# Splitting the first layer's input products by token halves and running its recurrence beside them

## The chip, the core and the metric

The kernel runs on one core of one Trainium2 chip, all in float32. Times are device microseconds of one launch. Before the change the median of three runs is 2656.42 us (2653.24 to 2658.45). TensorE is called PE in the profile, VectorE DVE, ScalarE ACT, GpSimd POOL and SyncE SP; TensorE's clock has two levels here, 1.2 and 2.4 GHz, given as a granted clock of 0.5 and 1.

## What is computed

The reference runs two transformer layers over 512 tokens of width 1024 and then a third block of another kind. The change lies in the first layer's mixer, a gated linear recurrence over chunks of 16 tokens with 8 heads of 128:

```python
proj = xn @ w_in                       # [512, 4096] = q | f | i | g
fgate = lbf + (1 - lbf) * sigmoid(f);  log_f = log(fgate);  k = 1 - fgate
q = silu(q);  v = i
def step(state, (qc, kc, vc, lfc)):    # one chunk of 16 tokens
    cum = cumsum(lfc);  last = cum[-1]
    qd, kd = qc * exp(cum), kc * exp(-cum)
    scores = where(causal, qd @ kd.T, 0)
    o = scores @ vc + qd @ state
    state = exp(last) * state + (kc * exp(last - cum)).T @ vc
o = o * rsqrt(mean(o * o) + eps) * onorm_g * silu(g)
h = h + gate * (o @ w_out)
```

`xn` is the normed input, scaled and shifted by columns of modulation vectors. All of these (17 x 1024 numbers) are products of the condition vector with matrices of 1024 rows; the kernel computes those of later layers beside the first layer's products too.

## The kernel before

The stages follow one another, each in a block with a barrier at its end. Within a block every engine runs its own list of instructions in order and waits for semaphores.

`first_loads` loads constants and `h`, and starts the first slabs of the modulation matrices (`vring`, GpSimd's DMA queue). `project` (L187) is the general routine: TensorE runs a list of jobs, each a group of matmuls into one PSUM bank with weights from a ring of three 2 MB slabs (`load_slab`, L160, on SyncE's queue), ScalarE or VectorE evacuates, and, where `vectors` is given, VectorE multiplies matrix slabs of 1024 x 256 by the condition vector (`vector_parts`, L291 and L295, eight instructions for a group of 256 columns), GpSimd reloads the ring of three 1 MB slabs (L182), and TensorE sums the 128 partitions of a finished group with one-column matmuls (`vector_sums`, L239). Eight groups of partial sums can be pending (`NPART`).

`project("mods_a")` makes the first two vectors, without jobs. `norm_to_xT` norms `h` and turns it into `xT` (channels on partitions). `project("hgrn_in")` runs 32 jobs of 512 columns over 8 slabs: q and f by channel (`by_column`, all 512 tokens moving), v and g by tile of 128 tokens (`by_token`), all evacuated by ScalarE; 60 vector groups lie beside them.

`hgrn` (L487) is the recurrence, four tiles of 128 tokens. A schedule by (tile, step), the same on all three engines, orders it: LOG (ScalarE's Ln of the gate), CUM (VectorE's scans and differences), EXPS (three Exp), PREP (VectorE multiplies them into q and keys), REACH to REACH+8 (VectorE builds the keys as seen from each chunk into one of three buffers, TensorE forms the chunk's scores of all heads, 16 passes), TURN (VectorE masks the scores, chain of chunk decays; TensorE turns the keys), OUT (TensorE's outputs and the state's increment, ScalarE's evacuation, VectorE's state), SUM, ROOT (Ln and Exp on ScalarE), GATE. The next tile's CUM to PREP is put between TURN and SUM of this one.

`turn_to_xT` transposes the gated output, `make_rows` spreads four gate vectors over the partitions (rows), and `project_back` runs 8 output jobs of 512 columns; VectorE adds them, gated, to `h` (L406, L407). Then come the experts and all the rest, which the change leaves as it is but for the numbers of two slabs in the ring.

## Time and profile before

| | us |
|---|---|
| median of the timed runs | 2656.42 |
| profiled execution | 2656.48 |
| its span in the trace | 2654.7 |
| TensorE busy | 2072.0 (78%) |
| VectorE busy | 1683.3 (63%) |
| ScalarE busy | 789.3 (30%) |
| GpSimd busy | 620.0 (23%) |
| end of the output products of the first layer | 541.8 |

A busy share is an average over stages with different limits; matmuls are pipelined, so that a busy TensorE isn't one at its peak. In a timeline line the first number is the start, the second the length of the merged group, "x16" the number of instructions in it, and what stands in brackets is the idle time before it and what ended that. A group of matmuls ends with the drain of its last one, about 0.17 us.

### The profile page before, as it was taken

To read this page: it belongs to the slowest core of one execution; us is meant where nothing else is said; L and a number is where in the kernel's file an instruction comes from. 1 tells how busy PE (TensorE), PEld (TensorE's weight loads), DVE (VectorE), ACT (ScalarE), POOL (GpSimd) and SP (SyncE) were. 2 spreads that over 40 slices of the span, in tenths; PEclk is the share of its full clock that TensorE was granted. 3 is DMA by queue.
4 is the path that set the end of the run, shared out by engine and by line. 5 is a ranking of instruction groups with operands and counts; after the bars stand their busy time and mean duration, and the time that the engine had idled before them with its cause. 6 is when DMAs were issued, how large, how long until landed. Compare 5 with 4: busy or idle time off the path is not lost. (4 is left out here: it accounts for less than half of the span.)

```text
span 2654.7 us, 30433 instructions
## 1 busy us (share of the span) xinstructions
PE 2072.0 (78%) x11214; PEld 1224.0 (46%) x11214; DVE 1683.3 (63%) x3993; ACT 789.3 (30%) x1736; POOL 620.0 (23%) x589
## 2 busy tenths in 40 slices
PE   2999776857776689888789888867887859856787
PEld 1454376443322146555256445523433436636664
DVE  5888875238978677554676753467885424954442
ACT  1100132123332332543343553335232242131221
POOL 0111000014444433433332233233344300000000
PEclk9999866979878699989799898877999969986889
DMA  7788600029999999999899888889999923310000
GB/s 299 286 315 326 239 1 1 32 96 421 420 419 421 422 416 413 407 391 387 358 371 392 302 333 302 337 351 350 420 418 419 420 104 112 93 74 1 9 9 16
DMA packets 111189, 723.58 MB, mean 273 GB/s; under 512 B 12080, under 2 KB 15024, under 8 KB 34880
## 3 DMA queue, kind: packets, MB, share of 16 engines
q0 software_dynamic: 84000, 610.65, 57.7%
q1 hardware_dynamic: 27040, 110.98, 11.1%
q8 instruction: 89, 1.46, 0.2%
q14 instruction: 60, 0.49, 0.0%
HBM read 718.18 MB, written 3.41 MB: 272 GB/s over the span
## 5 line engine op out<-in xcount | busy, mean ns | idle before, releaser
L1494 PE MATMUL ps<-got,diag 64*64 64x512 f32 x4096 | 640.1, 715 | 315.4 <-ACT diag L1565 293.5
L1515 POOL DMA_INDIRECT got<-in_peer_uv,idx x512 | 581.1, 1135 | 980.8 <-PE ps L1494 878.8
L1600 DVE CUSTOM_DVE_ANT_0 got<-got,xk 128x1024 f32<-128x1024 f32 x512 | 615.9, 1222 | 272.7 <-DMA got<-in_peer_uv,idx 262.3
L1494 PEld LDWEIGHTS ps<-got,diag 64*64 64x64 f32 x4096 | 127.5, 148 | 623.8 <-ACT diag L1565 516.6
L1560 ACT ACTIVATE gelu<-eye,hid 128x64 f32<-128x64 f32 x512 | 176.5, 345 | 689.3 <-DVE hid L1600 684.5
L1128 PE MATMUL ps<-xT,ring 128*128 128x256 f32 x928 | 225.3, 394 | 6.6 <-DVE qkv L1217 6.6
L1128 PEld LDWEIGHTS ps<-xT,ring 128*128 128x128 f32 x928 | 174.5, 194 | 85.5 <-issue 46.7
L295 DVE SCALAR_TENSOR_TENSOR hgrn_in_psums<-vring,vec,hgrn_in_psums 128x256 f32<-128x256 f32 x420 | 203.6, 485 | 15.0
L1565 ACT ACTIVATE diag<-gelu,gate 128x64 f32<-128x64 f32 x512 | 178.0, 348 | 54.6 <-PE ps L1494 6.6
L830 PE MATMUL ps<-xT,ring 128*128 128x256 f32 x768 | 190.2, 397 | 0.3 <-ACT xT L943 0.3
L830 PEld LDWEIGHTS ps<-xT,ring 128*128 128x128 f32 x768 | 144.0, 195 | 76.5 <-issue 47.1
L256 PE MATMUL ps<-ring,xT 128*128 128x512 f32 x384 | 169.0, 596 | 1.4 <-PEq L459 1.4
L859 PEld LDWEIGHTS ps<-ring,xT 128*128 128x128 f32 x1024 | 118.4, 192 | 44.8 <-issue 36.7
L859 PE MATMUL ps<-ring,xT 128*128 128x128 f32 x1024 | 128.9, 280 | 0.0
L256 PE MATMUL ps<-xT,ring 128*128 128x512 f32 x256 | 113.3, 597 | 1.2 <-PEq L356 1.2
L256 PEld LDWEIGHTS ps<-ring,xT 128*128 128x128 f32 x384 | 71.7, 190 | 85.9 <-issue 85.9
L182 POOL DMA_DIRECT2D vring<-in_vslabs x68 | 36.1, 532 | 271.6 <-DVE hgrn_in_psums L291 202.9
L256 PEld LDWEIGHTS ps<-xT,ring 128*128 128x128 f32 x256 | 47.6, 190 | 56.0 <-issue 56.0
L1471 PEld LDWEIGHTS ps<-xT,ring 128*128 128x128 f32 x512 | 59.9, 194 | 24.3 <-issue 17.0
L1471 PE MATMUL ps<-xT,ring 128*128 128x128 f32 x512 | 64.6, 282 | 2.4 <-PEq L356 1.2
L2129 PE MATMUL ps<-w_out,xT 128*128 128x512 f32 x128 | 61.2, 628 | 0.8 <-DVE xT L2275 0.8
L1506 POOL IOTA iota<- 128x16 f32 x1 | 0.1, 135 | 249.5 <-POOLq L356 249.5
(497 smaller groups left out, 2494.5 us busy)
## 6 DMA issues: line engine op xcount, KB each, us to landing
ring<-in_small SPq DMA_DIRECT2D x142, 512.0 KB
vring<-in_vslabs POOLq DMA_DIRECT2D x68, 1024.0 KB, 5.2
ring<-in_slabs SPq DMA_DIRECT2D x12, 2048.0 KB, 9.4
got<-in_peer_uv,idx POOLq DMA_INDIRECT x512
w_out<-in_slabs SPq DMA_DIRECT2D x2, 2048.0 KB, 11.0
h<-in_x SPq DMA_DIRECT2D x1, 2048.0 KB, 16.6
out<-h SPq DMA_DIRECT2D x4, 512.0 KB, 2.6
bias_rows<-brow POOLq DMA_DIRECT2D x1, 1280.0 KB, 4.8
```

The costliest lines, as they stand in the source:

```text
L256: mm = nc.tensor.matmul(o, l, r, start=start, stop=end)
L295: ins = nc.vector.scalar_tensor_tensor(acc, part, one, acc, ALU.mult, ALU.add)
L830: mm = nc.tensor.matmul(bank[:, 0:2 * P], w[:, k, :], xT[:, k, own], start=(k == 0), stop=(k == ND - 1))
L859: mm = nc.tensor.matmul(bank[:, P * half:P * half + P], x[:, k, P * half:P * half + P], w[:, k, :], start=(k == 0), stop=(k == ND - 1))
L1128: mm = nc.tensor.matmul(bank[:, 0:2 * P], w[:, k, :], xT[:, k, own], start=(k == 0), stop=(k == ND - 1))
L1471: mm = nc.tensor.matmul(ps[:, bank, P * half:P * half + P], slab(f + g)[:, k, c:c + P], xT[:, k, P * w:P * w + P], start=(k == 0), stop=(k ...
L1494: mm = nc.tensor.matmul(ps[to:to + HALF, i, :], diag[own, n % NDIAG, :], got[own, n % GRING, 1, 512 * g:512 * g + 512], start=(k == 0), st ...
L1515: nc.gpsimd.indirect_dma_start(out=got[:, n % GRING].rearrange("p a d -> p (a d)"), out_offset=None, in_=table, in_offset=bass.IndirectOff ...
L1560: nc.scalar.activation(gelu_of[:, n % 2, :], eye2[:], ACT.Gelu, scale=hid[:, w % 2, k:k + 1]).then_inc(gelu_done, 1)
L1565: nc.scalar.activation(diag[:, i, :], gelu_of[:, n % 2, :], ACT.Copy, scale=gate[:, w % 2, k:k + 1]).then_inc(diag_ready, 1)
L1600: nc.vector.tensor_tensor_reduce(row_in, row_in, xk[:, w % 2, :], 1.0, 0.0, ALU.mult, ALU.add, hid[:, w % 2, k:k + 1]).then_inc(dotted, 1)
L2129: mm = nc.tensor.matmul(ps[:, 4 * (t % 2) + 2 * part, :], xT[:, j, P * t:P * t + P], w_out[:, part, j, :], start=(j == 0), stop=(j == ND - 1))
```

## The change

- A vector group has 512 columns, not 256, and is loaded in four pieces of 2 x 128 rows (0.5 MB each); the ring holds five pieces, and two groups of partial sums can be pending.
- `hgrn_in` is cut in two. `in_a` runs 32 jobs of 256 columns for tokens 0 to 255 with 14 vector groups, `in_b` 32 such jobs for tokens 256 to 511 with 16 groups. The eight weight slabs are loaded twice.
- The recurrence is cut in halves of two tiles (`hgrn_half`), written as generators that give one step at a time on each engine. The next tile starts 12 steps after the last (`HGAP`). That of tiles 0 and 1 runs beside `in_b`: behind each job every engine does one step, TensorE one job later (`paced`). The products have three PSUM banks, the recurrence four, the vectors one. Its work tiles lie in parts of `xT`, `rows` and `h` that are free then.
- The recurrence of tiles 2 and 3 is a block of its own, into which `beside_hgrn` puts, at every second step, a step of `back_half` for tokens 0 to 255: one gate row, 16 transposes, and 4 output jobs in two chunks of 8 passes each. `h` is loaded again in that block, since it was used as work space.
- A last block makes the other three gate rows and the output jobs of tokens 256 to 511.
- Before its first Ln each half asks for the activation table set with logarithm and exponential.

```diff
-VCOLS = 256
-NVRING = 3
-NPART = 8
+VCOLS = 512
+VK = 2
+NVRING = 5
+NPART = 2
...
+    slabs = in0 + in0 + [q0[0], out0[0], out0[1], None, q0[1]]
+    OUT_SLABS, Q0_SLABS = (17, 18), (16, 20)
...
-                            for k in range(ND):
-                                one, part = cond[:, k:k + 1], vring[:, i % NVRING, k, :]
+                            for k in range(k0, k0 + VK):
+                                one, part = cond[:, k:k + 1], vring[:, i % NVRING, k - k0, :]
...
-            return [(bank[:, :T], w[:, k, c0:c0 + P], (xT if x is None else x)[:, k, :], k == 0, k == ND - 1)
-                    for k in range(ND)]
+            return [(bank[:, :2 * P], w[:, k, c0:c0 + P], xT[:, k, own], k == 0, k == ND - 1) for k in range(ND)]
...
+    def paced(side, lag):
+
+        made = []
+
+        def beside(eng, n):
+            if not made:
+                made.append(side(eng))
+            if n >= lag:
+                next(made[0], None)
+            if n == 31:
+                for _ in made[0]:
+                    pass
+        return beside
+
+    def beside_hgrn(mine, fill):
+
+        for s, _ in enumerate(mine):
+            if s >= 2 and s % 2 == 0:
+                next(fill, None)
+        for _ in fill:
+            pass
...
+                    if k == LOG:
+                        if u:
+                            act.wait_ge(cum_ready, u)
+                        else:
+                            nc.scalar.preload_act_table_set("natural_log_exp_and_others")
...
-            project("hgrn_in", jobs, range(first, len(vslabs)), take_mods(16, NMOD))
-        hgrn(q_all, f_all, v_all, g_all)
-        turn_to_xT("o0", v_all, v("onorm_g"))
-    make_rows()
-    project_back("hgrn_out", "hgrn_out", 0, first_of["out2"])
...
+            project("in_a", half_jobs(0), range(first, middle), take_mods(16, 16 + 4 * 14))
...
+                project("in_b", half_jobs(1), range(middle, len(vslabs)), take_mods(16 + 4 * 14, NMOD), beside=beside,
+                        banks=(4, 5, 6))
...
+                @block.tensor
+                def _(pe):
+                    beside_hgrn(side["pe"](pe), back["pe"](pe))
```

## Rows read from the trace of the kernel before

**Rows 1.** Busy time of each engine by stage; x counts instructions, PEclk is the granted clock.

```profile
core 0: us, PE busy (x) PEld busy (x) DVE busy (x) ACT busy (x) POOL busy (x), PEclk, DMA share, GB/s
0.00:19.30 19.30, 0.00 (x0) 0.00 (x0) 1.58 (x10) 1.72 (x3) 1.94 (x7) 1.00 0.79 303
19.30:51.90 32.60, 8.11 (x32) 7.42 (x32) 29.49 (x65) 0.00 (x0) 4.22 (x8) 1.00 0.69 239
51.90:66.90 15.00, 6.61 (x32) 5.49 (x32) 8.87 (x16) 8.39 (x12) 0.00 (x0) 1.00 1.01 430
66.90:320.90 254.00, 247.39 (x752) 124.73 (x752) 220.50 (x481) 22.96 (x35) 30.16 (x57) 0.99 0.81 304
320.90:467.20 146.30, 93.14 (x696) 90.53 (x696) 103.74 (x270) 49.05 (x51) 0.00 (x0) 0.59 0.00 1
467.20:483.60 16.40, 12.30 (x48) 7.91 (x48) 7.81 (x8) 6.85 (x8) 0.00 (x0) 0.89 0.00 0
483.60:541.80 58.20, 55.17 (x128) 24.24 (x128) 11.06 (x16) 0.00 (x0) 0.00 (x0) 1.00 0.10 36
541.80:2654.70 2112.90, 1649.27 (x9526) 963.65 (x9526) 1300.26 (x3129) 700.37 (x1627) 583.72 (x517) 0.87 0.74 295
```

**Rows 2.** Groups by line and shape, whole run: busy us, mean ns, idle before.

```profile
L291 DVE TENSOR_SCALAR hgrn_in_psums<-vring,vec 128x256 f32<-128x256 f32 x60 | 20.9, 348 | 17.1 <-DMA vring<-in_vslabs 16.7 <-PEq L356 0.4
L295 DVE SCALAR_TENSOR_TENSOR hgrn_in_psums<-vring,vec,hgrn_in_psums 128x256 f32<-128x256 f32 x420 | 203.6, 485 | 15.0
L1802 DVE SCALAR_TENSOR_TENSOR score<-rel,sb_z,score 128x512 f32<-128x512 f32 x7 | 5.3, 752 | 4.3 <-ACT rel L1785 4.1
```

**Rows 3.** Timeline of TensorE, four places: start, length, what, idle before.

```profile
311.55 1.40 PE L239 MATMUL ps<-const,hgrn_in_psums 128*128 128x1 f32 x12
390.44 1.95 PE L599 MATMUL ps<-v_all,hg_kend 128*128 128x128 f32 x16
483.78 55.17 PE L256 MATMUL ps<-ring,xT 128*128 128x512 f32 x128 [1.42 <-PEq L459]
2285.78 31.35 PE L1128 MATMUL ps<-xT,ring 128*128 128x256 f32 x144 [1.73 <-DVE qkv L1217]
```

**Rows 4.** Busy time by stretch inside the recurrence, columns as in the first group.

```profile
320.90:336.20 15.30, 0.00 (x0) 0.00 (x0) 13.75 (x33) 10.20 (x9) 0.00 (x0) 0.50 0.00 0
336.20:353.50 17.30, 17.26 (x136) 17.11 (x137) 13.25 (x42) 2.95 (x3) 0.00 (x0) 0.50 0.01 1
353.50:388.00 34.50, 25.21 (x184) 24.36 (x183) 29.57 (x79) 13.54 (x14) 0.00 (x0) 0.60 0.00 1
```

**Rows 5.** Timeline of the recurrence: tile 0's start, the step between tiles, the end.

```profile
321.10 1.00 DVE L609 TENSOR_SCALAR f_all<-f_all,lb 128x512 f32<-128x512 f32 x2 [0.61 <-PEq L207]
325.95 1.28 ACT L540 ACT_TABLE_LOAD   x1
326.46 2.63 DVE L623 TENSOR_TENSOR_SCAN xT<-hg_starts,xT 128x128 f32<-128x128 f32 x8
336.24 15.77 PE L570 MATMUL ps<-xT,hg_reach 128*16 128x16 f32 x128 [16.07 <-DVE hg_reach L655]
380.17 1.31 DVE L663 COPY_PREDICATED hg_scores<-imask,ps 128x1024 f32<-128x1024 int32 x1 [1.44 <-issue]
414.89 1.31 DVE L663 COPY_PREDICATED hg_scores<-imask,ps 128x1024 f32<-128x1024 int32 x1 [1.44 <-issue]
449.33 1.29 DVE L663 COPY_PREDICATED hg_scores<-imask,ps 128x1024 f32<-128x1024 int32 x1 [7.72 <-issue]
465.81 1.22 DVE L693 TENSOR_TENSOR v_all<-q_all,g_all 128x1024 f32<-128x1024 f32 x1
```

**Rows 6.** Timeline of TensorE in the expert stage, where its clock falls.

```profile
1895.03 1.99 PE L1128 MATMUL ps<-xT,ring 128*128 128x256 f32 x8
1900.77 1.95 PE L1494 MATMUL ps<-got,diag 64*64 64x512 f32 x8 [2.73 <-ACT diag L1565]
1902.65 2.77 PE L1128 MATMUL ps<-xT,ring 128*128 128x256 f32 x8
```

More of the change, by code:

```diff
@@ L99, in vector_plan @@
     wide = [("ada_w", 0, 6), ("ada_w", 1, 6), ("kv_ada_w", None, 2), ("w_ada_2", 0, 3)]
-    return [(name, layer, c) for name, layer, n in wide for c in range(0, n * D, VCOLS)]
+    return [(name, layer, c, k) for name, layer, n in wide for c in range(0, n * D, VCOLS) for k in range(0, ND, VK)]
 def program(nc, io, out):
@@ L182, in load_vslab, with project @@
             eng.dma_start(vring[:, i % NVRING].rearrange("p k n -> p (k n)"), io["vslabs"][i]).then_inc(v_loaded[i % NVRING], 16)
-    NBANK = 6
-    def project(name, slab_jobs, vectors=(), after=None, beside=None, until=None):
+    def project(name, slab_jobs, vectors=(), after=None, beside=None, banks=range(6)):
         jobs = [(i, job) for i, js in slab_jobs for job in js]
@@ L308, in _ @@
                             dve.wait_ge(filled, n + 1)
-                            evac(nc.vector, ps[:, n % NBANK, :], step).then_inc(dve_out, 1)
+                            evac(nc.vector, ps[:, banks[n % NBANK], :], step).then_inc(dve_out, 1)
                         if beside:
@@ L400, in _ @@
                         mm.then_inc(turned, 1)
-    def add_gated(row):
-        def make(t, c0, tmp):
-            def evac(eng, bank, step):
-                step(eng.tensor_tensor(tmp[:, :], bank[:, :WCOLS], rows[:, row, c0:c0 + WCOLS], ALU.mult))
-                return eng.tensor_tensor(h[:, t, c0:c0 + WCOLS], h[:, t, c0:c0 + WCOLS], tmp[:, :], ALU.add)
-            return evac
-        return make
-    def project_back(name, key, row, until):
-        with ExitStack() as st:
-            tmp = sbuf(st, name + "_tmp", [P, WCOLS])
-            make = add_gated(row)
-            first = first_of[key]
-            project(name, [(first + g, [(by_token(t, 0, WCOLS), "dve", make(t, WCOLS * g, tmp)) for t in range(NT)])
-                           for g in range(2)], until=until)
     def root(act, n, x, root_in, root_mid, root_out):
@@ L2348, in build @@
         g_all = sbuf(st, "g_all", [P, NT, D])
+        own_tiles = {n: sbuf(st, "hg_" + n, [P, H, P])[:] for n in ("state", "scores", "kend", "reach0")}
         with ExitStack() as st_v:
-            vring = sbuf(st_v, "vring", [P, NVRING, ND, VCOLS])
+            vring = sbuf(st_v, "vring", [P, NVRING, VK, VCOLS])
             first_loads()
@@ new lines, in build @@
+            project("in_a", half_jobs(0), range(first, middle), take_mods(16, 16 + 4 * 14))
+            with ExitStack() as st_a:
+                quarter = lambda x, t: x[:, :, P * t:P * t + P]
+                flat_tile = lambda x: x.rearrange("p (h x) -> p h x", h=H)
+                tl = dict(own_tiles, logf=quarter(xT, 0), cum=quarter(xT, 1))
+                tl |= {n: flat_tile(rows[:, i, :]) for i, n in enumerate(("ke0", "qd1", "kd1", "ke1"))}
+                tl |= {n: flat_tile(h[:, i, :]) for i, n in enumerate(("qd0", "kd0", "reach1", "reach2"))}
+                side = hgrn_half(st_a, 0, tl, q_all, f_all, v_all, g_all)
+                beside = {}
+                for e, lag in (("pe", 1), ("act", 0), ("dve", 0)):
+                    beside[e] = paced(side[e], lag)
+                project("in_b", half_jobs(1), range(middle, len(vslabs)), take_mods(16 + 4 * 14, NMOD), beside=beside,
+                        banks=(4, 5, 6))
@@ new lines, in build, with _ @@
+        with ExitStack() as st_b:
+            tl = dict(own_tiles, logf=quarter(xT, 2), cum=quarter(xT, 3), qd0=quarter(q_all, 0), kd0=quarter(q_all, 1),
+                      ke0=quarter(f_all, 0), qd1=quarter(f_all, 1), kd1=flat_tile(g_all[:, 0, :]), ke1=flat_tile(g_all[:, 1, :]))
+            tl |= {n: sbuf(st_b, "hg_" + n, [P, H, P])[:] for n in ("reach1", "reach2")}
+            h_again, = sems(st_b, "h_again")
+            side = hgrn_half(st_b, 1, tl, q_all, f_all, v_all, g_all)
+            back = back_half(st_b, 0, v_all, [0], h_again)
+            with nc.Block(no_gpsimd_drain=True) as block:
+                @block.sync
+                def _(sp):
+                    sp.dma_start(h[:], io["x"][0].rearrange("(t p) d -> p t d", p=P)).then_inc(h_again, 16)
+                    sp.wait_ge(h_again, 16)
+                @block.tensor
+                def _(pe):
+                    beside_hgrn(side["pe"](pe), back["pe"](pe))
+                @block.scalar
+                def _(act):
+                    beside_hgrn(side["act"](act), back["act"](act))
+                @block.vector
+                def _(dve):
+                    beside_hgrn(side["dve"](dve), back["dve"](dve))
@@ new lines, in build, with _ @@
+        with ExitStack() as st_c:
+            back = back_half(st_c, 1, v_all, [1, 2, 3], None)
+            with nc.Block(no_gpsimd_drain=True) as block:
+                @block.sync
+                def _(sp):
+                    sp.wait_ge(back["job_done"], 2)
+                    load_slab(sp, OUT_SLABS[0] + NRING)
+                @block.tensor
+                def _(pe):
+                    for _ in back["pe"](pe):
+                        pass
+                @block.scalar
+                def _(act):
+                    for _ in back["act"](act):
+                        pass
+                @block.vector
+                def _(dve):
+                    for _ in back["dve"](dve):
+                        pass
```

588 lines of the change are left out of this document (313 added, 275 removed).

## The prediction

> **What bounds the kernel now.** I first cut the run into the blocks that the code forms and read busy time and granted clock in each [rows 1]. The profiled execution took 2656.48 us, 1.78 more than its span of 2654.7; the median of the three timed runs is 2656.42, so a sum against the profiled run needs no correction. The change touches what ends at 541.8 us; the 2112.9 us behind it keep their instructions and are carried over unchanged. Ahead of it stand seven stages: loads 19.3, first modulation vector 32.6, norm 15.0, input products 254.0, recurrence 146.3, turning plus gate rows 16.4, output products 58.2, together 541.8. The reader is to see three things. The input products are bound by TensorE: 247.4 of 254.0 us busy at full clock, with VectorE at 220.5 beside it on the vector products. The recurrence is bound by nothing that is full: TensorE 93, VectorE 104, ScalarE 49 of 146.3 us, at a granted clock of 0.59. It is a chain that hops between engines. The output products are TensorE alone, 55.2 of 58.2. So overlap has something to win: in 146 us the array does little, and in 254 + 58 us VectorE and ScalarE have room, if VectorE's vector products are made cheaper.
>
> **Unit costs at full clock.** A 512-column pass takes 0.430 us ((55.17 - 0.17)/128; 0.17 is the last one's drain) and a 256-column pass (31.35 - 0.17)/144 = 0.2165 [rows 3]. An f32 matmul is two passes. Hence halving the width costs almost nothing: 1024 narrow passes are 221.7 us where 512 wide ones are 220.0. A half-size job of 16 passes is 3.46 us. A vector column sum is 0.11 us a pass: 1.40 us for 12 [rows 3]; four per old group of 256 columns, eight per new group of 512, so 30 new groups cost what 60 old ones did, 0.89 us each. On VectorE an old group is one 348 ns and seven 485 ns instructions [rows 2], 3.9 us with gaps (the vector stage holds eight in 32.6 us less its 1.3 us tail [rows 1]). The same operation at 512 columns takes 752 ns [rows 2]; with 0.48 for the first (taken between 348 ns and 500 ns, the L609 form over 512 [rows 5]) and small gaps a new group is 5.9 us, 34 of them 201 us where 68 old took 265.
>
> **Part 1, loads and first vector.** The loads block ends when h has landed, and everything in flight shares the rate of 303 GB/s [rows 1]. The new ring holds 5 x 0.524 MB, not 3 x 1.049 MB, so 0.5 MB less lies ahead: -1.7 us, 17.6. The vector stage is 4 x 5.9 + 1.3 = 24.9 if transfers keep up. That asks 0.524 MB per 1.48 us, 354 GB/s, against 239 at a DMA share of 0.69 now, and slab loads start four pieces before the end. I take 25.5 (24.9 to 30). The norm stays 15.0.
>
> **Part 2, input products of tokens 0 to 255.** TensorE: 512 x 0.2165 + 14 groups x 0.89 = 110.8 + 12.5 = 123.3, plus 1.2 of tail. VectorE: 14 x 5.9 = 83, hidden. The transfers are the doubt: 56 vector pieces (29.4 MB) and 8 slabs (16.8 MB, the slabs being loaded twice now) are 46.1 MB, 374 GB/s over 123 us. The input stage now moves 304 GB/s at a share of 0.81, which scales to 375, but the norm's window shows 430 [rows 1]. Only two groups of partial sums are buffered instead of eight, and VectorE already loses 16.7 us to late vector slabs [rows 2]. I take 127 (124 to 136).
> The Trainium skill's page "DMA: Bandwidth & Descriptors", section Specifications, puts the HBM limit of a core at about 358 GB/s; by it the stage would take 46.1/358 = 129 us, an estimate, 2 us over my value. The 430 GB/s row speaks against a limit there.
>
> **Part 3, products of tokens 256 to 511 with the recurrence of tiles 0 and 1.** Products and sums: 110.8 + 16 x 0.89 = 125.0. TensorE's share of the recurrence: at half clock tile 0's 128 score passes take 15.8 us [rows 5], so 7.9 at full; turning, output and state products are 16-pass blocks of 1.8 us at full clock (1.95 for 16 with drain [rows 3]), the turn half of it; tile 0 makes 12.5, tile 1, with a product against the state, 14.4. Sum 152 us. VectorE: 16 x 5.9 = 94.4, and its part of two tiles is 13.75 + 13.25 + 29.6 = 56.6, the busy time from 320.9 to 388.0 [rows 4]: sum 151. Two engines near 150 us that wait for each other step by step: each VectorE job with an even number waits for TensorE's sums of the job before, and TensorE runs step s after job s+1. Walking through the pairs of jobs (TensorE 7.8 us + steps, VectorE 5.9 us + steps) gives three losses. At the start VectorE owes gates and memsets 4.1, scan and differences 5.0, gated keys 3.9 and three pairs' pieces before the first score: it is ready at 28, TensorE at 22.5, 5.5 us. Between the tiles TensorE waits for state copy 1.2, sum 1.4, keys 3.9 and two jobs' pieces 5.9, of which two jobs cover all but 5 us. At the end the last groups and the lag cost 6 to 7 us. Together 170. ScalarE's evacuations (0.4 us) hide; three product banks in place of six suffice, because evacuation runs at most three jobs late in the walk.
> Then the clock. In the expert stage 256-column blocks take 1.99 us, but behind a gap of 2.73 us the next two blocks take 1.95 in place of 1.09 and 2.77 [rows 6]. In the recurrence the score passes leave the clock at 0.50 although TensorE reads 17.26 of 17.3 us busy [rows 4]: narrow passes don't hold it up. Beside the products a score step plus sums is a gap of 1 to 2.5 us between dense jobs, so some falls are likely. Each costs about 1 to 2 us; I take six, 9 us: 179. Bounds are 168 (no fall, fewer waits) and 200.
>
> **Part 4, the block with tiles 2 and 3 and the first output products.** A two-tile recurrence from the present rows: start to the end of the first tile's scores 31.1 (320.9 to 336.24 + 15.77), mask to mask 34.7 (380.17 to 414.89), last mask to end 17.9 (449.33 to 467.2) [rows 5], 83.7. Put into it: 4 output jobs, eight chunks of 8 wide passes, 3.44 us each at full clock; one gate row, 1.7; 16 transposes, 2.6. Of the chunks the one before each mask (VectorE has 4.7 us there), the one behind each output product and the last are covered; four stand in the score steps, where TensorE is full (17.26 of 17.30) [rows 4], 13.8 us bare. That gives 83.7 + 13.8 + 4.3 + 2 of VectorE work = 104; chunks that begin at half clock add some 7, score passes that meet a warm array return 3: 108 (96 to 130). The h reload of 2 MB, now 16.6 us to landing beside others, hides.
> One part is worth 2 to 4 us on paper: each Ln and each Exp reloads its table, 1.28 us [rows 5], twice in a tile's tail. The Trainium skill's "ScalarE: Activation LUTs", section "Table sets: the hidden batching unit", says that one set holds both functions; the new preload asks for it. If that holds, some 3 us leave this block, an estimate; I leave them out of the sum.
>
> **Part 5, the last block.** Three gate rows through one buffer, 3.05 each + 1.1 = 10.3; transposes and evacuation 4.4; 4 jobs x 6.87 = 27.5; last add and block end 3.8: 46 (44 to 50). It replaces, with part 4, the 16.4 and 58.2 of now.
>
> **Sum.** 17.6 + 25.5 + 15.0 + 127 + 179 + 108 + 46 = 518.1, against 541.8: -23.7. 2656.5 - 23.7 = 2632.8, predicted 2633.
>
> **The rivals.** *A, smooth overlap*: clock full throughout, transfers in time: 17.6 + 24.9 + 15 + 124.5 + 169 + 98 + 45 = 494, 2609. For it: VectorE's steps are known and the products are dense. Against: [rows 6]. *B, transfers bind*: the first half takes 136, the vector stage 29, the second half 182: +15.5, 2648. For it the share of 0.81 at 304 GB/s, against it 430 GB/s. *C, overlap in name only*: the engines are coupled in order, each step waits for its slowest partner, and half of the hidden work comes back: second half 190, part 4 120: +23, 2656. The change doesn't do what it says. *D, slower*: the clock falls beside the products. TensorE's 152 us of the second half at a mean clock c last 152/c; with 18 us of waits and c = 0.76 that is 218, and part 4 at half clock throughout 125 (+17): 2689 in full. The total passes 2656 where these two together exceed my values by 24, about c = 0.85. The expert stage with its gaps shows 0.87 [rows 1], which makes this real; against it, TensorE has work nearly always here, and the product stage shows 0.99.
>
> **How the numbers follow.** Forecast 0.55 (2622 to 2648); A 0.17; B 0.10; C 0.08; D 0.10. 0.2%, 5.3 us, is about what a measurement of this kernel can tell from no change. Slower by more takes D: 0.10. Within: C and a little of B: 0.09. Faster: 0.81. The range leaves out part of A below and most of D above: 2602 to 2664.
>
> **What would show it.** The first half at 123 to 130 us with TensorE above 95% busy; wide pass time unchanged; vector groups of 5.9 us. In the second half TensorE above 85% and a granted clock above 0.9; if it is below 0.85, D. In part 4 scores and wide chunks alternating, the block near 108. A long wait for vector pieces in front of L291's successor would be B. If the stages behind move by more than 3 us, the carry-over was wrong.

## The result and the profile after

The changed kernel takes 2617.77 us (median of four runs, 2616.77 to 2626.79) against 2654.83 of the kernel before beside it (2647.89 to 2658.45): a ratio of 0.9871, 95% interval 0.9841 to 0.9901. The predicted 2633 lay on the right side and the time is within the range, but 15 us too high; the time falls below the forecast's own band (2622 to 2648), between it and rival A's 2609. The profiled execution took 2617.68 us and has a span of 2615.7, 39.0 less than before.

Busy time by stage of the changed kernel, columns as in [rows 1]. The stages are loads, first vector, norm, first half of the products, second half with tiles 0 and 1, tiles 2 and 3 with the first output products, the last block, and all the rest.

```profile
core 0: us, PE busy (x) PEld busy (x) DVE busy (x) ACT busy (x) POOL busy (x), PEclk, DMA share, GB/s
0.00:18.30 18.30, 0.00 (x0) 0.00 (x0) 1.57 (x9) 1.71 (x3) 2.98 (x9) 1.00 0.78 291
18.30:46.70 28.40, 7.46 (x32) 7.12 (x32) 22.88 (x33) 0.00 (x0) 8.47 (x16) 1.00 0.83 303
46.70:61.80 15.10, 7.01 (x32) 5.92 (x33) 8.85 (x15) 8.42 (x13) 0.00 (x0) 1.00 0.96 402
61.80:188.10 126.30, 123.92 (x624) 110.59 (x625) 80.21 (x113) 16.07 (x35) 29.59 (x56) 0.99 0.92 348
188.10:368.10 180.00, 164.27 (x992) 146.20 (x992) 143.35 (x267) 45.73 (x65) 31.41 (x59) 0.94 0.76 279
368.10:465.80 97.70, 71.42 (x428) 49.72 (x428) 60.01 (x155) 17.50 (x23) 0.00 (x0) 0.78 0.06 22
465.80:514.30 48.50, 39.22 (x92) 16.85 (x92) 10.87 (x15) 4.64 (x8) 0.00 (x0) 0.89 0.12 44
514.30:2615.70 2101.40, 1641.20 (x9526) 959.29 (x9526) 1302.20 (x3129) 697.63 (x1625) 581.73 (x517) 0.87 0.74 297
```

| stage | before | forecast | measured |
|---|---|---|---|
| loads | 19.3 | 17.6 | 18.3 |
| first vector | 32.6 | 25.5 | 28.4 |
| norm | 15.0 | 15.0 | 15.1 |
| products, first half | 254.0 for all | 127 | 126.3 |
| second half, tiles 0 and 1 | 146.3 (four tiles) | 179 | 180.0 |
| tiles 2 and 3, first outputs | 16.4 (turning, rows) | 108 | 97.7 |
| last block | 58.2 (outputs) | 46 | 48.5 |
| sum | 541.8 | 518.1 | 514.3 |
| the rest | 2112.9 | 2112.9 | 2101.4 |

So of the 39.0 us in the span 27.5 come from the stages that the change touches (23.7 forecast) and 11.5 from stages whose work it leaves alone (none forecast).

**The second half.** The reader is to see TensorE 91% and VectorE 80% busy in the fifth line: both chains are in there and neither waits much. What TensorE and VectorE waited for in it (us in total, times, longest), first TensorE, then VectorE:

```profile
PE ps L479 <- DVE hg_reach L561: 9.2, 2, 5.0
PE ps L239 <- DVE in_b_psums L296: 5.7, 1, 5.7
```

```profile
DVE in_b_psums L292 <- PE ps L239: 13.4, 6, 2.7
...
DVE in_b_psums L296 <- DMA vring<-in_vslabs: 1.2, 1, 1.2
```

TensorE's three waits are the three of the forecast: before the first scores, between the tiles (two in the first row, 4.14 and 5.04 in the timeline, 5.5 and 5 forecast) and at the tail (5.7; 6 to 7 forecast). VectorE waits for TensorE's sums (L239) six times: each waits on the other, as the walk had it. Transfers cost 1.2 us.

The same stage in stretches of 10 us, columns as before (five of its eighteen):

```profile
188.10:198.10 10.00, 9.97 (x36) 8.42 (x37) 9.13 (x19) 3.96 (x4) 1.58 (x3) 0.77 0.85 342
208.10:218.10 10.00, 5.86 (x42) 4.98 (x40) 8.52 (x12) 0.77 (x2) 2.12 (x4) 0.92 0.96 379
218.10:228.10 10.00, 10.00 (x49) 8.28 (x49) 9.40 (x20) 0.38 (x1) 2.95 (x6) 0.74 0.87 301
288.10:298.10 10.00, 10.00 (x59) 8.08 (x59) 9.51 (x16) 0.76 (x2) 2.11 (x4) 0.82 0.53 197
298.10:308.10 10.00, 10.00 (x74) 8.80 (x72) 8.08 (x18) 0.72 (x3) 2.71 (x5) 1.00 1.00 401
```

The granted clock is below 1 at the block's start, during and behind each of the two waits of 4 to 5 us, in the stretch in which the second of them lies (0.84, row not shown) and in the last (0.76, not shown). In all other stretches it is 1.00, those with score passes of 16 columns between products of 256 among them.

**The block with tiles 2 and 3**, in four stretches: until the first score, first scores to the first mask, mask to second scores, second scores to the second mask. (The end, 16.8 us at a clock of 1.00, isn't shown.)

```profile
368.10:383.00 14.90, 0.00 (x0) 0.00 (x0) 11.76 (x32) 5.29 (x5) 0.00 (x0) 0.50 0.39 141
383.00:404.00 21.00, 20.28 (x149) 17.96 (x149) 9.69 (x28) 3.64 (x6) 0.00 (x0) 0.58 0.00 1
404.00:424.00 20.00, 15.57 (x87) 10.24 (x88) 17.25 (x45) 6.21 (x8) 0.00 (x0) 0.84 0.01 1
424.00:449.00 25.00, 25.00 (x154) 15.37 (x151) 10.48 (x27) 0.00 (x0) 0.00 (x0) 0.92 0.00 1
```

TensorE does nothing in the first, stands at half clock in the second (scores, transposes, one row, no wide chunk), and near full clock in the fourth, where four wide chunks lie between the scores. The chunks in the timeline of TensorE, the first, one of the score stretch and the last:

```profile
404.00 5.51 PE L668 MATMUL ps<-ring,xT 128*128 128x512 f32 x8
...
424.15 5.69 PE L668 MATMUL ps<-ring,xT 128*128 128x512 f32 x8
...
457.37 3.60 PE L668 MATMUL ps<-ring,xT 128*128 128x512 f32 x8
```

Two of the eight begin at half clock and take 5.5 and 5.7 us, the other six 3.6 to 3.7. The four between the second tile's scores are those that begin at 424.15, 431.20, 437.03 and 443.42.

**The last block**, timeline of TensorE:

```profile
467.08 3.78 PE L647 MATMUL ps<-hb_spread,const 128*128 128x512 f32 x4 [6.12 <-DVE hb_spread L695]
472.18 3.78 PE L647 MATMUL ps<-hb_spread,const 128*128 128x512 f32 x4 [1.32 <-DVE hb_spread L695]
477.29 1.98 PE L647 MATMUL ps<-hb_spread,const 128*128 128x512 f32 x4 [1.32 <-DVE hb_spread L695]
480.38 1.97 PE L654 MATMUL ps<-const,v_all 128*128 128x128 f32 x16 [1.11 <-ACT rows L679]
483.71 27.71 PE L668 MATMUL ps<-ring,xT 128*128 128x512 f32 x64 [1.36 <-issue]
```

Three gate rows by turns: two at half clock (3.78 us for four passes), the third at full (1.98). The output products that follow take 27.7 us, 0.430 a pass as in [rows 3].

**The vector groups** of the first half (busy us, mean ns, idle before and what ended it):

```profile
L296 DVE SCALAR_TENSOR_TENSOR in_a_psums<-vring,vec,in_a_psums 128x512 f32<-128x512 f32 x98 | 73.6, 751 | 21.7 <-DMA vring<-in_vslabs 15.5 <-DVE in_a_psums L296 0.5
L292 DVE TENSOR_SCALAR in_a_psums<-vring,vec 128x512 f32<-128x512 f32 x14 | 6.8, 484 | 22.4 <-PE ps L239 11.8 <-DMA vring<-in_vslabs 10.2 <-PEq L356 0.4
```

751 and 484 ns are the 752 and 480 of the forecast. In the first half VectorE stood 25.7 us (15.5 + 10.2) waiting for late pieces, and it cost nothing, since TensorE was busy for 123.9 of 126.3 us.

### The profile page after: what moved, and what is told of

It reads as the page before. It is cut to its first block and busy times, and to the rows that moved or that the text cites. A ratio compares the mean times of both kernels' runs of the same rounds, so it can differ in the third digit from the quotient of the medians.

```text
span 2615.7 us, 31361 instructions
## 1 busy us (share of the span) xinstructions
PE 2054.5 (79%) x11726; PEld 1295.7 (50%) x11726; DVE 1629.9 (62%) x3736; ACT 791.7 (30%) x1770; POOL 654.2 (25%) x657
## 5 line engine op out<-in xcount | busy, mean ns | idle before, releaser
L1151 PE MATMUL ps<-xT,ring 128*128 128x256 f32 x928 | 226.5, 396 | 6.6 <-DVE qkv L1240 6.6
L1151 PEld LDWEIGHTS ps<-xT,ring 128*128 128x128 f32 x928 | 175.3, 195 | 86.4 <-issue 48.3
L853 PE MATMUL ps<-xT,ring 128*128 128x256 f32 x768 | 188.6, 395 | 0.3 <-ACT xT L966 0.3
L853 PEld LDWEIGHTS ps<-xT,ring 128*128 128x128 f32 x768 | 142.9, 193 | 76.2 <-issue 47.3
L184 POOL DMA_DIRECT2D vring<-in_vslabs x136 | 72.2, 532 | 282.9 <-DVE in_b_psums L296 137.8
L882 PEld LDWEIGHTS ps<-ring,xT 128*128 128x128 f32 x1024 | 118.5, 192 | 44.6 <-issue 36.5
L256 PE MATMUL ps<-xT,ring 128*128 128x256 f32 x512 | 119.5, 393 | 2.1 <-PEq L356 1.2
L256 PE MATMUL ps<-ring,xT 128*128 128x256 f32 x512 | 117.3, 387 | 0.0
L256 PEld LDWEIGHTS ps<-xT,ring 128*128 128x128 f32 x512 | 99.2, 197 | 16.0 <-issue 2.4
L256 PEld LDWEIGHTS ps<-ring,xT 128*128 128x128 f32 x512 | 97.2, 193 | 12.7
L296 DVE SCALAR_TENSOR_TENSOR in_b_psums<-vring,vec,in_b_psums 128x512 f32<-128x512 f32 x112 | 84.1, 751 | 8.2 <-DMA vring<-in_vslabs 1.2
L296 DVE SCALAR_TENSOR_TENSOR in_a_psums<-vring,vec,in_a_psums 128x512 f32<-128x512 f32 x98 | 73.6, 751 | 21.7 <-DMA vring<-in_vslabs 15.5
L1493 PEld LDWEIGHTS ps<-xT,ring 128*128 128x128 f32 x512 | 60.4, 195 | 23.8 <-issue 16.5
L668 PE MATMUL ps<-ring,xT 128*128 128x512 f32 x128 | 60.8, 630 | 1.4 <-issue 1.4
## 6 DMA issues: line engine op xcount, KB each, us to landing
got<-in_peer_uv,idx POOLq DMA_INDIRECT x512, 12.5
h<-in_x SPq DMA_DIRECT2D x2, 2048.0 KB, 11.7
```

What stands on the lines that cost most here:

```text
L256: mm = nc.tensor.matmul(o, l, r, start=start, stop=end)
L296: ins = nc.vector.scalar_tensor_tensor(acc, part, one, acc, ALU.mult, ALU.add)
L853: mm = nc.tensor.matmul(bank[:, 0:2 * P], w[:, k, :], xT[:, k, own], start=(k == 0), stop=(k == ND - 1))
L882: mm = nc.tensor.matmul(bank[:, P * half:P * half + P], x[:, k, P * half:P * half + P], w[:, k, :], start=(k == 0), stop=(k == ND - 1))
L1151: mm = nc.tensor.matmul(bank[:, 0:2 * P], w[:, k, :], xT[:, k, own], start=(k == 0), stop=(k == ND - 1))
L1493: mm = nc.tensor.matmul(ps[:, bank, P * half:P * half + P], slab(Q0_SLABS[g])[:, k, c:c + P], xT[:, k, P * w:P * w + P], start=(k == 0), s ...
```

## The experiments

The theory: the gain is two overlaps, each worth more than the halving costs; TensorE and VectorE bound the second half together. The rivals: the gain is the cheaper vector products or the table preload (then the vector format alone has it), the overlap is in name only, or transfers bind.

**The vector format alone.** The kernel before with groups of 512 columns, pieces of 0.5 MB, and nothing else.

```diff
-VCOLS = 256
-NVRING = 3
-NPART = 8
+VCOLS = 512
+VK = 2
+NVRING = 5
+NPART = 2
```

> The kernel before with nothing but the new vector format (groups of 512 columns, four pieces, ring of five, two pending sums). My theory: the vector block loses what the changed kernel's trace shows, 32.6 to 28.4 us and 1.0 us in the loads block, and the input products, bound by TensorE, keep their 254 us less a shorter tail of 2 to 4 us. So 2655 - 8 = 2647 (2643 to 2651). Rival: the cheaper VectorE work by itself carries much of the gain, since the input stage was held by late vector slabs (16.7 us of waits there): then 2635 or below.

It took 2648.97 us, a ratio of 0.9983 (0.9971 to 0.9996): 2.5 us between the medians, 4.5 by the ratio, about as expected. In its trace the front ends at 537.6 instead of 541.8: the first vector takes 27.2 in place of 32.6, the products 253.9 in place of 254.0. The shorter tail that was expected there didn't show. The products were TensorE's, so cheaper work on VectorE gained nothing; it is what makes room for the recurrence.

**The recurrence of tiles 0 and 1 behind the second half.** The changed kernel, where the second half's products run alone and a block of their own holds the two tiles.

```diff
-                project("in_b", half_jobs(1), range(middle, len(vslabs)), take_mods(16 + 4 * 14, NMOD), beside=beside,
+                project("in_b", half_jobs(1), range(middle, len(vslabs)), take_mods(16 + 4 * 14, NMOD),
                         banks=(4, 5, 6))
+                with nc.Block(no_gpsimd_drain=True) as block:
+                    @block.tensor
+                    def _(pe):
+                        for _ in side["pe"](pe):
+                            pass
...
```

> The changed kernel, with the recurrence of tiles 0 and 1 in a block of its own behind the second half's products. My theory: the products fall from 180 to 127 us, and a block of 80 to 84 us comes in: +29, 2647 (2640 to 2655). Rival (overlap in name only): each step waits for its slowest partner and the overlap returns little; then the time stays within 10 us of the changed kernel.

2658.75 us, 1.0023 (1.0009 to 1.0037): slower than before, and above the 2640 to 2655 expected. The two blocks, columns as before, and VectorE's waits for transfers in the first:

```profile
186.50:327.70 141.20, 131.35 (x640) 115.98 (x640) 91.33 (x129) 14.83 (x34) 31.18 (x59) 0.95 0.94 356
327.70:411.80 84.10, 48.79 (x352) 47.69 (x352) 53.71 (x138) 15.82 (x19) 0.00 (x0) 0.58 0.01 2
```

```profile
DVE in_b_psums L296 <- DMA vring<-in_vslabs: 28.4, 8, 6.4
DVE in_b_psums L292 <- DMA vring<-in_vslabs: 10.7, 4, 5.1
```

The two take 225.3 us, beside each other 180.0. The front ends at 555.6, 41.3 later than in the changed kernel. That rules out the overlap in name only. But the products alone take 141.2, not the some 127 that TensorE's work asks for, which is why the expectation was missed: at a DMA share of 0.94 VectorE waits 39 us for pieces. That suggests that this stage, run at TensorE's own pace, is bound by transfers; the rival is that the two pending groups of sums bind it.

**The same with half of the vector traffic of that stage.** From there on every second piece is loaded only in the first 64 columns of one of its two row blocks. All instructions on the engines stay; what the kernel leaves out is data, so that those modulation vectors aren't the reference's.

```diff
+            if i >= 77 and i % 2:
+                eng.dma_start(vring[:, i % NVRING, 0, 0:64], io["vslabs"][i][:, 0:64]).then_inc(v_loaded[i % NVRING], 16)
+                return
```

> The kernel of e2 (recurrence of tiles 0 and 1 alone), in which every second piece of the vector matrices from the second half's products on is loaded only in its first 64 columns of one row block, so those modulation vectors are wrong. In e2 the second half's products took 141 us where TensorE's work is 127, with 39 us of VectorE waits for vector pieces at 356 GB/s. Theory: transfers bind that block; with 15 MB less it falls to 127 to 129 us. Rival: the two pending sums bind it (TensorE and VectorE wait in turn); then it stays near 141.

A single run, 2650.81 us, so the whole time says little; the stage is what counts. The second half's products:

```profile
186.00:315.00 129.00, 127.60 (x640) 113.54 (x640) 92.14 (x130) 14.86 (x34) 31.87 (x59) 0.98 0.73 264
```

129.0 us, TensorE 127.6 of it, 12 us less than above with the same instructions on the engines. So it was the transfers, since the two groups of sums are the same here. Overlapped, the two stages are 45.3 us shorter (225.3 against 180.0; at the front's end it is 41.3, since the stages around them take 4 us less in the trace of the kernel that runs them apart). Some 12 of these are the transfers': with the recurrence beside them they have 180 us for the same bytes. The engines' share is 33 (129.0 + 84.0 against 180.0). Of it about 10 are TensorE's own work becoming shorter, 127.6 + 46.6 us busy apart and 164.3 together: the recurrence alone runs at a clock of 0.58, beside the products the stage has 0.94. The other 23 are idle time that is filled.

**The output products of tokens 0 to 255 in a block of their own**, behind tiles 2 and 3.

```diff
-                    beside_hgrn(side["pe"](pe), back["pe"](pe))
+                    for _ in side["pe"](pe):
+                        pass
...
+            with nc.Block(no_gpsimd_drain=True) as block:
+                @block.tensor
+                def _(pe):
+                    for _ in back["pe"](pe):
+                        pass
...
```

> The changed kernel, with the output products of tokens 0 to 255 in a block of their own behind the recurrence of tiles 2 and 3. My theory: the recurrence alone takes 80 us at a clock near 0.6 (it is 97.7 with them), the outputs alone 36: +18, 2636 (2630 to 2642). Second question: if the wide chunks hold the clock up in the score steps, the block with them should owe less than the 13.8 + 4.3 us that I put on top of the recurrence; then the recurrence alone is nearer 85 than 80.

2644.83 us, 0.9974 (0.9964 to 0.9984), above the 2630 to 2642 expected, because both blocks are longer than the 80 and 36 us assumed; in the trace the front ends at 536.0, 21.7 later. The block of tiles 2 and 3, twenty microseconds of its second score stretch, the new block and the last:

```profile
366.00:452.00 86.00, 46.09 (x344) 45.01 (x344) 52.02 (x142) 14.80 (x18) 0.00 (x0) 0.58 0.07 25
412.00:431.00 19.00, 11.74 (x109) 11.56 (x109) 12.99 (x29) 0.53 (x3) 0.00 (x0) 0.51 0.00 0
452.00:490.70 38.70, 33.16 (x84) 14.98 (x84) 8.41 (x13) 2.60 (x5) 0.00 (x0) 0.94 0.00 0
490.70:536.00 45.30, 35.62 (x92) 15.85 (x92) 10.88 (x15) 4.67 (x8) 0.00 (x0) 0.99 0.13 47
```

The two tiles alone take 86.0 (83.7 was the forecast's base), with the outputs between them 97.7: 38.7 us of other work added 11.7. The scores alone stand at a clock of 0.51; with wide chunks between them their stretch has 0.92. These lines give the second tile's scores, first alone, then with chunks:

```profile
416.95 0.61 PE L479 MATMUL ps<-f_all,hg_reach 128*16 128x16 f32 x16 [7.86 <-DVE hg_reach L561]
419.87 15.35 PE L479 MATMUL ps<-f_all,hg_reach 128*32 128x16 f32 x112 [2.31 <-DVE hg_reach L561]
```

```profile
423.61 0.61 PE L479 MATMUL ps<-f_all,hg_reach 128*16 128x16 f32 x16 [4.43 <-DVE hg_reach L561]
```

Alone they take 18.3 us from the first to the last, 2.3 of it a wait for VectorE, and with four chunks 25.2 (they end at 448.8): 6.9 more, though the four chunks take 16.8. The first tile's stretch is 5.3 longer with a row and the transposes in it (21.1 against 15.8); the pieces between and behind change by under 1 us.

The 97.7 itself isn't fixed. The same block takes 97.6 in the second trace of the changed kernel and 94.8 to 95.7 in three of four traces of kernels that differ only ahead of it, where the clock comes up again within the first tile's scores and they take 18 us to their mask, not 21. The two tiles alone take 87.5 in the trace with both overlaps taken out. So what the outputs add is 7 to 12 us. The last block is 3.2 us shorter here (45.3), at a clock of 0.99: the block ahead of it ends with wide products.

**Both in blocks of their own.** The two edits above together.

> The changed kernel with both overlaps taken out (recurrence of tiles 0 and 1 and the first output products in blocks of their own); only the halves and the vector format remain. If the two gains add, it is the changed kernel's 2618 + 41 (e2) + 27 (e3) = 2686, well above the 2651 of the kernel before. Rival: they share a cause (the clock, the transfers), and the time is under 2676.

2687.24 us, 1.0141 (1.0111 to 1.0172). That is the 2686 expected. The two overlaps add up: in the traces' fronts they return 41.3 and 21.7 taken out one by one, 66.8 (581.1 - 514.3) taken out together. Without them the change is a loss. Against the vector format alone the front is 43.5 us longer (581.1 - 537.6). The input products then take 10 us more (124.0 + 140.3 against 253.9), the recurrence in two halves 23 more (84.4 + 87.5 against 148.7), and what is behind 9 more.

**Without the preload of the table set.**

```diff
                         else:
-                            nc.scalar.preload_act_table_set("natural_log_exp_and_others")
```

> The changed kernel without the request for the activation table set with Ln and Exp. In the changed trace no table is loaded in tile 3's tail nor in the norm that opens the expert stage. My theory: two loads of 1.28 us come back in each of these two places, all others hidden: +5, 2623 (2621 to 2626). Rival: the norm's loads vanished for another reason and the tail's are hidden: no difference.

2621.43 us, 0.9886 (0.9869 to 0.9902); the medians are 3.7 us apart. ScalarE's timeline without it, at the start of the block of tiles 2 and 3, in tile 3's tail and in the next stage's norm (each load at L405 is followed by a second one for the Exp at L407):

```profile
371.29 1.06 ACT L446 ACTIVATE xT<-f_all 128x1024 f32<-128x1024 f32 x1 [1.47 <-DVE f_all L515]
...
456.67 1.28 ACT L405 ACT_TABLE_LOAD   x1
...
513.27 1.28 ACT L405 ACT_TABLE_LOAD   x1
```

and with it:

```profile
370.83 1.28 ACT L447 ACT_TABLE_LOAD   x1 [11.48 <-DVE f_all L517]
372.12 1.06 ACT L448 ACTIVATE xT<-f_all 128x1024 f32<-128x1024 f32 x1
...
461.00 0.21 ACT L405 ACTIVATE hg_ss<-hg_ss 128x8 f32<-128x8 f32 x1 [1.49 <-DVE hg_ss L590]
...
517.10 0.20 ACT L405 ACTIVATE p_ss<-p_ss 128x4 f32<-128x4 f32 x1 [0.47 <-DVE p_ss L380]
```

The loads are gone, but they were worth little in the front: it ends at 510.9 without the preload and at 514.3 with it. The preload stands behind ScalarE's wait for the gates, so its 1.28 us lie on the chain: the first Ln begins 4.0 us after VectorE's first gate instruction (at 368.13), without it 2.7 (after 368.58), since there the load runs at 368.53, during the wait. Between the tiles VectorE waits 0.6 us for the last Exp without the preload and not with it. In the tail the root's Exp begins 2.75 us after ScalarE's last square, without the preload 4.03. So the block gains 0.6 us net. What stays is the norm behind the touched stages, which uses the same two functions: from its start to the Exp of its root 3.1 us in place of 5.2, so 2.1 of the rest's 11.5. That the front ends 3.4 us sooner without the preload is the clock's doing: the first tile's scores take 18.1 us to their mask here and 21.2 in the changed kernel, but 18 in three traces with the preload as well, and one gate row less of the last block meets half clock (1.8 us). The 3.7 between the medians is within the intervals of both. In the half beside the products the preload saves nothing: there Silu for the products' evacuations reloads its own set in between, and both kernels have the same number of loads.

**Four pieces in flight and three groups of sums** in place of five and two (five and three weren't tried).

```diff
-NVRING = 5
-NPART = 2
+NVRING = 4
+NPART = 3
```

> The changed kernel with three pending partial sums and a vector ring of four pieces, not two and five. In the second half VectorE waits 13.4 us for TensorE's sums and TensorE 14 us for VectorE, which I put down to the coupling through two pending sums. Theory: with one more sum VectorE can run two jobs further ahead and part of the 14 us goes: -3 to -6 there; the smaller ring costs the first half, at the edge of the transfers, 0 to 5. Rival: the waits come from VectorE's own work (151 us of it in steps), then nothing is won and the smaller ring makes it 3 to 8 us slower.

2640.92 us, 0.9954 (0.9937 to 0.9971), 23 us above the changed kernel's median. A gain of 3 to 6 us in the second half was expected for the third group of sums, and a loss of up to 5 in the first, up to 8 in all by the rival; both were far off. First vector, first half, second half, and VectorE's waits for transfers in the first half:

```profile
16.00:52.30 36.30, 7.47 (x32) 7.12 (x32) 22.97 (x33) 0.00 (x0) 8.46 (x16) 1.00 0.85 311
67.40:201.90 134.50, 127.47 (x625) 112.25 (x625) 79.65 (x115) 16.11 (x35) 29.60 (x56) 0.97 0.88 323
201.90:391.00 189.10, 167.11 (x992) 147.93 (x992) 143.53 (x268) 45.74 (x65) 31.93 (x60) 0.92 0.75 271
```

```profile
DVE in_a_psums L296 <- DMA vring<-in_vslabs: 42.4, 16, 7.4
```

Each of the three stages is 8 to 9 us longer. One piece less in flight lowers the first half's rate from 348 to 323 GB/s and turns 15.5 us of hidden waits into 42.4, which now show. In the second half VectorE's waits for pieces rise from 1.2 to 15.7, and TensorE's wait before the first scores from 4.1 to 8.1. The third group of sums won nothing visible; two things were changed at once, so its own effect isn't shown.

**Two vector groups moved from the second half to the first** (16 and 14).

```diff
-            middle = first + 14 * pieces
+            middle = first + 16 * pieces
```

> The changed kernel with 16 vector groups in the first half and 14 in the second, not 14 and 16. Theory from e2: 348 to 356 GB/s is all that these two kinds of transfer reach here, and the first half with 46 MB in 126 us stands at that edge; 4.2 MB more makes it 12 us longer, while the second half loses two groups of VectorE and TensorE work there, 5 to 8 us: +4 to +7. Rival: VectorE is the bound of the second half and the first has room; then it is 6 us or more faster.

2621.39 us, 0.9903 (0.9878 to 0.9929). Both halves:

```profile
61.50:205.70 144.20, 128.57 (x640) 113.38 (x640) 91.50 (x130) 16.11 (x35) 34.14 (x64) 0.95 0.92 348
205.70:377.30 171.60, 161.15 (x976) 143.13 (x976) 131.84 (x251) 45.74 (x65) 27.12 (x51) 0.95 0.71 255
```

The second half gains 8.4 us, the first loses 17.9 at the same 348 GB/s as in the changed kernel: 8 more pieces are 4.2 MB, 12 us at that rate, as expected; the other 6 aren't accounted for. TensorE idles 15.6 us of the first half here, 2.4 in the changed kernel: with 14 groups transfers and TensorE take about the same time, with 16 the transfers bind. The front is 7.2 us longer. The medians differ by 3.6, the times against the kernel before beside each (2649.46 and 2654.83) by 9.0, and the intervals of the two ratios overlap, so the whole time doesn't settle it. This trace's rest is the shortest of all (2095.0); more on that below.

**All four gate rows in the head of the block of tiles 2 and 3**, one at every second step from its first, none in the last block.

```diff
-            if s >= 2 and s % 2 == 0:
+            if s % 2 == 0:
                 next(fill, None)
...
-            back = back_half(st_b, 0, v_all, [0], h_again)
+            back = back_half(st_b, 0, v_all, [0, 1, 2, 3], h_again)
...
-            back = back_half(st_c, 1, v_all, [1, 2, 3], None)
+            back = back_half(st_c, 1, v_all, [], None)
```

> The changed kernel with all four gate rows made in the block of tiles 2 and 3, one at each of its steps 0, 2, 4 and 6, where TensorE idles for 15 us and VectorE waits for ScalarE. The last block then opens with the transposes: its three rows cost 14.6 us in the changed trace. Theory: the last block loses 14, the other gains 3 to 6: -8 to -11, 2608. Rival: VectorE's spreads stand on the chain of the recurrence's start and TensorE runs them at half clock; then the block grows by 12 us and nothing is won.

2604.35 us, 0.9843 (0.9816 to 0.987), a little better than the 2608 expected. Both blocks and the start of the first:

```profile
365.50:463.00 97.50, 77.63 (x440) 47.85 (x440) 63.64 (x158) 20.35 (x26) 0.00 (x0) 0.81 0.06 22
463.00:498.00 35.00, 31.00 (x80) 15.00 (x80) 7.26 (x12) 1.70 (x5) 0.00 (x0) 0.95 0.17 60
```

```profile
369.92 3.78 PE L647 MATMUL ps<-hb_spread,const 128*128 128x512 f32 x4 [5.24 <-DVE hb_spread L696]
```

Three rows more in the block with tiles 2 and 3, and it isn't longer (97.5 against 97.7), because two of the four (at 369.92 and 376.91) lie where TensorE had nothing. The last block falls from 48.5 to 35.0.

**That and a distance of 11 steps between tiles** in place of 12.

```diff
-    HGAP = 12
+    HGAP = 11
```

> The kernel of e8 with the second tile of each half starting 11 steps behind the first, not 12, so that its scans no longer stand in the same step as the first tile's mask (8 us of VectorE in one step). Theory: the stall between the tiles (5.0 us in the second half) shrinks to 1 to 3 and the block of tiles 2 and 3 loses up to 3: -2 to -6 against e8, 2600. Rival: the scan moves ahead of the mask and delays it; no change or slower.

2615.07 us, 0.9865 (0.984 to 0.9889), front 503.6 against 498.0. A gain of 2 to 6 us was expected. But TensorE's wait between the tiles is no shorter (5.3 us, 5.0 with 12 steps), and its waits for vector sums rise from 5.7 to 10.3. Nothing won.

**The changed kernel and the one with early rows once more, side by side.**

> The changed kernel once more, for its time beside e8 on one chip and for a second trace. Its stages up to the expert stage should take 514 us within 3, and the rest, the same code as before, anything from 2095 to 2113, the span that the traces so far show.

> The kernel of e8 beside the changed kernel on one chip. Theory: the stages ahead of the experts take 498 us against 514, so the medians differ by 10 to 18 us. Rival: the 13 us between the medians of separate calls were the expert stage's own spread; then they differ by less than 5.

2616.4 (0.9855, 0.9835 to 0.9874) and 2605.66 (0.9817, 0.9798 to 0.9835) on one chip, against 2654.98 of before. Early rows are 10.7 us faster by medians, within the 10 to 18 expected; no run of one kernel overlaps with one of the other (2611.53 to 2617.16 and 2597.17 to 2608.65), and the fronts end at 512.9 and 496.8. This version beats both kernels.

## Why the prediction was right, and where it was off

**The direction and the second half: right, for the reasons given.** TensorE's 152 us at full clock, 18 of waits and 9 of clock made 179. Measured are 15.7 idle and 164.3 busy, 12.3 over the 152, so 180.0. The waits stand where the walk put them. The 12.3 put the cost of the clock a little above the 9 forecast, and the falls have another pattern: not the small gaps at score steps, which I had counted as six likely falls, but only the block's start and what lies in and behind TensorE's three real waits. Rival D wanted a mean clock under 0.85; it was 0.94. Rival C is refuted by the 41 us that the overlap returns, B by 126.3 in the first half and 1.2 us of waits in the second.

**The first half: right, and nearer to B than I thought.** TensorE's 123.9 are the 123.3 of the sum. I leaned on the norm's 430 GB/s [rows 1] to hold B small. The products' stages didn't come near that: 348 GB/s at a share of 0.92, 356 at 0.94 with the recurrence moved away. There the row that counted was [rows 1]'s own product line, 304 at 0.81, which scales to 375. It went well by little: two vector groups more, and TensorE idles 15.6 us. As a rate to plan these stages with, the about 358 GB/s for a core in the Trainium skill's "DMA: Bandwidth & Descriptors", section Specifications, fits the trace (348 and 356) better than my 430 does, though it isn't a limit: stretches of the second half show 379 and 401, the norm 402. The time fell on my side all the same, 127 against its 129, since the stage moved 348 x 126.3 = 44.0 MB and not 46.1; the rest must have come ahead of it, by the ring's first pieces and slabs.

**Halving the width is nearly free: right.** A pass is one matmul record of the trace, of which an f32 matmul leaves two. 512 passes of 256 columns and 14 groups of sums fit in the 123.9 us that 0.2165 us a pass gave.

**The first vector, mis-sized by 2.9 us.** A group takes 6.1 us, not 5.9: seven instructions of 751 ns follow each other in steps of 0.823 in the timeline, a gap of 0.07 us that I had taken as small from the 256-column groups. Four groups are 24.5, late pieces cost 1.3, and the tail of sums is 2.5 rather than 1.3.

**Part 4, the term that was most wrong: 97.7, not 108.** The base alone takes 86.0 where 83.7 was forecast. Its start and its tail are 0.3 and 1.2 us shorter than the rows of before gave, but from mask to mask it takes 38.5 (396.82 to 435.31) and not 34.7: TensorE waits 7.9 us for VectorE before the second tile's scores, where the kernel before, with its own order of steps, showed 2.8 (at 395.15).

On top I had put 24 us: 13.8 for four chunks in the score steps, less 3 for score passes that meet a warm array, 7 for chunks that begin at half clock, and 4.3 and 2 for the rest. Measured are 11.7, so this term was some 12.5 too high. The step that failed is the one in the score steps, where the sum had 13.8 - 3 + 7 = 17.8 and the traces show 6.9, in three parts. TensorE isn't full in the second tile's score steps: the 17.26 of 17.30 us that I leaned on is the first tile's, and 2.3 us of wait are there to be filled. Only two of eight chunks begin at half clock, 2 us longer each, and the first of them lies beside the mask; it delays the outputs by 1 us, which then run 1.9 shorter at full clock. And the chunks raise the clock for the scores between them by more than the 3 us: without the wait the scores take 16.0 alone, and 8.4 between the chunks (25.2 - 16.8). The row, the transposes and the rest cost the other 4.8, where 6.3 were forecast. As the block's length goes by 3 us with the clock from trace to trace, these figures hold for this pair of traces.

The tables that I left out of the sum would have been wrong in it: some 3 us were to leave this block, and by the traces with and without it the preload puts 1.3 on its head and takes 0.6 from between its tiles and 1.3 from its tail. The Trainium skill's "ScalarE: Activation LUTs", section "Table sets: the hidden batching unit", says that one set holds both functions, and the trace agrees with it: after the load at 370.83 there is none for either until the norm is done.

**The last block, mis-sized by 2.5 us.** The rows cost 14.6 and not 10.3: I had them at 3.05 each from a kernel in which they followed one another at full clock, and two of three met half clock here (3.78 against 1.98 us for the same passes, 3.6 us for both; only one did in the trace without the preload). Transposes (3.3 against 4.4) and end (2.9 against 3.8) were shorter.

**The rest: the carry-over was wrong by 11.5 us.** It was to move by 3 us at most. 2.1 are the norm's tables. The other 9 lie in stages whose instructions are the same. Over the traces of this study the rest takes 2112.8, 2109.9 and 2108.7 us in the three kernels without the preload and 2095.0 to 2108.5, on average 2102.9, in the eleven with it. So the same code differs by 13 us from one trace to the next even among the eleven, and the trace of before is the longest of fourteen. Laid side by side by VectorE's instructions, before has lost 3.4 us against the changed kernel 596 us behind the front's end, 7.2 at 642 and 11.0 at 991, and it stays within some 2 us of that; other traces lose at other places. Why is open. Those stages are ones of gathers that TensorE, VectorE and transfers share (share 0.85 to 0.96 in stretches of 200 us between 1100 and 1900), and the runs don't tell whether the start time, the phase of the clock or something else decides, nor whether it is chance that all three without the preload lie above all eleven with it.

So how near the forecast came is in part luck. Without the rest it would have been 4 us off, but only because part 4, 10.3 too high, stood against terms that were 6.5 too low together.

## What to carry to other kernels

A stage bound by a chain of small steps and one bound by a full engine are worth overlapping when the unit beside which the chain runs has room on every engine that the chain needs. Here it had it on VectorE only after the vector products had been made cheaper, a step that is worth 4 us by itself. Splitting work to make an overlap possible costs (43 us here), so sum the split's price and the overlap's return apart. Part of the return is the clock: the recurrence's own matmuls become shorter beside a stage that keeps the granted clock at 1. When a stage gets shorter while its bytes stay, compare bytes over the new time with the rate that this same mix of transfers reaches, not with the best rate of any stage. When a load or a setting is moved ahead to save time, put it before the wait and not behind it. Then look where the full engine stands idle in the new order and put its small leftovers there: three rows of that kind were 11 us.

## What the runs showed of the hardware

Matmuls of 16 moving columns don't hold up TensorE's clock, and wider ones between them do it for both: the scores alone stand at a granted clock of 0.50 (TensorE busy for 17.26 of 17.30 us) and 0.51, between products of 256 columns at 1.00, and between chunks of 512 columns at 0.92. Score steps of 0.6 to 1.9 us between products went with no fall at all; idle waits of 4.1 and 5.0 us did, and the stretches behind them show 0.74 and 0.82.

What is in flight set the rate of these stages: a ring of four pieces of 0.5 MB, with the slabs beside it, moved 323 GB/s where one of five moved 348, at shares of 0.88 and 0.92. (The number of pending sums was changed with it.)

A table set that holds both Ln and Exp stays loaded on ScalarE through copies and squares, into the norm of another block: from 370.83 on there is no further load in the touched stages, nor the two of 1.28 us in the norm. It doesn't stay where Silu comes between.
